# Attention: row-maximum products of 64 rows in two row groups, with the key bias added by VectorE while it takes the maximum over two PSUM banks

## The reference: what is computed

```python
def fox_block(q, k, v, fq, fk, q_pos, k_pos):
    s = jnp.einsum('bqhd,bkhd->bhqk', q, k, preferred_element_type=jnp.float32) * ATTN_SCALE
    s = s + (jnp.transpose(fq, (0, 2, 1))[..., :, None] - jnp.transpose(fk, (0, 2, 1))[..., None, :])
    mask = k_pos[None, :] <= q_pos[:, None]
    s = jnp.where(mask[None, None], s, -jnp.inf)
    p = jax.nn.softmax(s, axis=-1)
    return jnp.einsum('bhqk,bkhd->bqhd', p.astype(v.dtype), v)
```

## Time and profile before

| | |
|---|---|
| median of 3 runs | 3664.59 us (3661.96 to 3668.26) |
| the profiled execution | 3662.56 us, its span 3660.9 us |
| attention phase, first to last product | 1128.9 to 2576.0 us of the span |
| TensorE busy, share of the span | 92% |
| VectorE, ScalarE, GpSimd | 45%, 29%, 36% |

### The profile page before, as it was taken

One profiled execution on the slowest core, in us unless ns is written; L12 is line 12 of the kernel. 1 busy time (PEld: TensorE's weight loads), 2 busy tenths in 40 slices (PEclk: granted clock), 3 DMA queues, 4 the chain that ended last, 5 costly groups with the idle time before them and its releaser, 6 DMA issues. The chain is left out here.

```text
span 3660.9 us, 49247 instructions
## 1 busy us (share of the span) xinstructions
PE 3355.1 (92%) x17784; PEld 2379.2 (65%) x17784; DVE 1656.8 (45%) x2644; ACT 1073.9 (29%) x1451; POOL 1334.9 (36%) x1273
## 2 busy tenths in 40 slices
PE   7999999796965999999999999999699999959998
PEld 5777777572823666666666666665377777748877
DVE  3223332262615655555555555553334443345554
ACT  4222222131311544545444445454200000001111
POOL 0000000033331888787878787878100000000000
PEclk9999999898985999999999999999799999979999
DMA  5333334399987113132232323110311111055664
GB/s 171 122 127 115 127 119 152 120 361 373 379 321 146 41 36 82 46 72 59 58 65 59 73 47 82 35 27 10 130 46 46 57 57 69 23 157 183 206 200 158
DMA packets 238130, 435.33 MB, mean 119 GB/s; under 512 B 63543, under 2 KB 105528, under 8 KB 235871
## 3 DMA queue, kind: packets, MB, share of 16 engines
q1 hardware_dynamic: 217191, 364.96, 32.8%
q0 software_dynamic: 20768, 68.17, 4.9%
HBM read 314.19 MB, written 119.03 MB: 118 GB/s over the span
## 5 line engine op out<-in xcount | busy, mean ns | idle before, releaser
L931 DVE TENSOR_REDUCE at_max_parts<-at_mx 128x1 f32<-128x512 f32 (+3 forms) x1152 | 736.6, 646 | 411.0 <-PE at_mx L991 284.7
L874 ACT ACTIVATE at_probs<-at_st,at_gap 128x1024 f32<-128x1024 f32 x448 | 498.2, 1114 | 511.5 <-PE at_st L1021 511.2
L840 POOL TENSOR_TENSOR at_pair_sum<-at_probs 128x1024 f32<-128x1024 f32 x224 | 531.2, 2372 | 196.7 <-ACT at_probs L874 180.2
L1041 PE MATMUL at_o_ps<-at_probs,at_v 128*64 128x512 f32 (+3 forms) x2304 | 499.8, 566 | 0.0
L991 PE MATMUL at_mx<-at_k_one,at_q_top 71*128 71x512 f32 (+3 forms) x1152 | 461.8, 402 | 14.4 <-DMA at_k_all<-scratch_k_parts 8.2
L1020 PE MATMUL at_st<-at_q_all,at_k_all 128*128 128x512 f32 (+3 forms) x1152 | 459.4, 399 | 6.9 <-ACT at_probs L878 5.6
L1021 PE MATMUL at_st<-at_q_one,at_k_one 67*128 67x512 f32 (+3 forms) x1152 | 440.4, 382 | 0.0
L93 PE MATMUL ga_acc<-ga_h_high,ga_w_high 128*128 128x512 f32 x768 | 311.7, 406 | 23.3 <-DVE ga_h_low L1285 21.0
L1041 PEld LDWEIGHTS at_o_ps<-at_probs,at_v 128*64 128x64 f32 x2304 | 171.8, 137 | 246.1 <-issue 185.3
L94 PE MATMUL ga_acc<-ga_h_low,ga_w_high 128*128 128x512 f32 x768 | 307.2, 400 | 0.0
L95 PE MATMUL ga_acc<-ga_h_high,ga_w_low 128*128 128x512 f32 x768 | 307.2, 400 | 0.0
(11 more groups left out here) (305 smaller groups left out, 4992.8 us busy)
## 6 DMA issues: line engine op xcount, KB each, us to landing
dc_pages<-in_cache_k_dram SPq DMA_DIRECT2D x128, 256.0 KB, 5.5
dc_pages<-in_cache_k_dram POOLq DMA_DIRECT2D x128, 256.0 KB, 5.3
dc_pages<-in_cache_v_dram SPq DMA_DIRECT2D x128, 256.0 KB, 7.6
dc_pages<-in_cache_v_dram POOLq DMA_DIRECT2D x128, 256.0 KB, 5.3
pj_x<-in_x_prompt_dram SPq DMA_DIRECT2D x32, 512.0 KB, 4.2
scratch_h_t<-pj_h_t SPq DMA_DIRECT2D x8, 2048.0 KB, 9.7
scratch_q_parts<-pj_stage SPq DMA_DIRECT2D x32, 512.0 KB, 3.3
scratch_k_parts<-pj_stage SPq DMA_DIRECT2D x32, 512.0 KB, 2.7
```

The costliest lines, as they stand in the source:

```text
L840: chain.link(nc.gpsimd.tensor_tensor(pair, first, second, ALU.add))
L874: nc.scalar.activation(probs[:, s % RING], st[:, s % 2], ACT.Exp, bias=bias).then_inc(exp_done, 1)
L931: nc.vector.tensor_reduce(max_parts[:, b % AHEAD, t, c:c + 1], mx[:, n % 2, 0:width], AX_X, ALU.max).then_inc(bank_done, 1)
L1041: last = nc.tensor.matmul(o_ps[half * HD:(half + 1) * HD, b % 2, at:TILE], v[:, h % 2, 4 * c + own], probs[:, s % RING, half, at:TILE], st ...
```

## The change

The key bias leaves the products. A unit is now up to two key tiles wide: two products of 64 rows, one with q's high part at partitions 0 to 63 (`q_all[0:64]`, keys from `k_one`), the other with the copy at partitions 64 to 127 (`q_all[64:128]`, keys from `k_all`, whose two halves change places), into the two banks of `mx`. VectorE reads both banks in one `tensor_tensor_reduce`, which adds `k_bias` (the key bias of the head, the same row in all 128 partitions, loaded by a DMA that repeats it), writes the sum back and gives the maximum. `q_top` and its loads go. A unit that takes both banks waits for the end of the use before it. The lists of units per group are remade (at most 5, or 4 on the diagonal). `combine` becomes two operations, the second of which also applies the tile's forget sum. The memsets of `k_one[HD:P]` and `q_top` go. `f_rows` has three rows in place of four, the third the full running sum. The ring of sums has six kept slots and one passing one.

```diff
-            PER = 4 + TT
+            PER = 3 + TT
...
-                chain.link(nc.vector.tensor_scalar(f_parts[:, 2], f_ones, f_past[:], None, ALU.mult))
+                chain.link(nc.vector.tensor_scalar(f_parts[:, 2].bitcast(F32), f_sum[:], -1.0, f_past[:], ALU.mult, ALU.add))
...
-                chain.link(nc.vector.scalar_tensor_tensor(out=f_parts[:, 3], in0=f_ones, scalar=f_past[:], in1=f_parts[:, 2].bitcast(F32),
-                                                          op0=ALU.mult, op1=ALU.subtract))
...
-    SUMS = 12
+    SUMS = 6
...
+    units = [(b, t, c, min(2, row(b) + 1 - c)) for b in range(NB) for t in range(TT) for c in range(0, row(b) + 1, 2)]
+    unit_base = [sum(1 for u in units if u[0] < b) for b in range(NB + 1)]
...
-        return 7 if g >= quad_base[NT] // 2 and (on_diagonal(2 * g) or on_diagonal(2 * g + 1)) else 9
+        return 4 if g >= quad_base[NT] // 2 and (on_diagonal(2 * g) or on_diagonal(2 * g + 1)) else 5
...
+        places = {1: (4,), 2: (0, 4), 3: (0, 3, 6), 4: (0, 3, 5, 8), 5: (0, 2, 4, 6, 8)}[len(here)] if here else ()
...
+    def width_of(b, t, c, n):
+
+        return n * TILE if c + n <= row(b) else (n - 1) * TILE + (t + 1) * P
...
+    kept = [n for n in range(NQUAD) if not summed_with_next(n)]
+
+    def sum_slot(n):
+
+        return SUMS if summed_with_next(n) else kept.index(n) % SUMS
...
                 sp.dma_start(k_one[h % 2][0:HD, cols].bitcast(F32), high).then_inc(k_loaded[h % 2][c], 16)
-                sp.dma_start(k_all[h % 2][0:HD, cols].bitcast(F32), high).then_inc(k_loaded[h % 2][c], 16)
-                sp.dma_start(k_all[h % 2][HD:P, cols].bitcast(F32), low).then_inc(k_loaded[h % 2][c], 16)
+                sp.dma_start(k_all[h % 2][HD:P, cols].bitcast(F32), high).then_inc(k_loaded[h % 2][c], 16)
+                sp.dma_start(k_all[h % 2][0:HD, cols].bitcast(F32), low).then_inc(k_loaded[h % 2][c], 16)
+                if h >= 2 and c == 0:
+                    sp.wait_ge(bank_done, bank_of["unit", unit_base[(h - 1) * NT] - 1] + 1)
+                sp.dma_start(k_bias[h % 2][:, cols], io["f_rows"][h, 2:3, cols].to_broadcast([P, KCHUNK])).then_inc(k_bias_loaded[h % 2][c], 16)
...
-                sp.dma_start(q_top[0:HD, n].bitcast(F32), high).then_inc(q_loaded[n], 16)
-                sp.dma_start(q_top[MINUS:KM, n].bitcast(F32), io["f_rows"][h, 2:4, cols]).then_inc(q_loaded[n], 16)
...
-                link(nc.vector.memset(t[HD:P].bitcast(F32), -1.0))
                 link(nc.vector.memset(t[HD:HD + 1].bitcast(F32), 1.0))
-            link(nc.vector.memset(q_top[HD:P].bitcast(F32), 1.0))
-            link(nc.vector.memset(q_top[HD:HD + 1].bitcast(F32), 0.0))
...
+                if k == unit_base[b] and j % 2 == 0:
+                    dve.wait_ge(k_bias_loaded[h % 2][j // 2], (h // 2 + 1) * 16)
+                dve.wait_ge(bank_ready, bank_of["unit", k] + 1)
+                both = mx[:].rearrange("p n t -> p (n t)")[:, 0:width]
+                nc.vector.tensor_tensor_reduce(out=both, in0=both, in1=k_bias[h % 2][:, c * TILE:c * TILE + width], scale=1.0, scalar=NO_MAX,
+                                               op0=ALU.add, op1=ALU.max, accum_out=max_parts[:, b % AHEAD, t, c // 2:c // 2 + 1]).then_inc(bank_done, 1)
...
-                nc.vector.tensor_reduce(shift_w[:, b % 2, :, HD], max_parts[:, b % AHEAD, :, 0:j + 1], AX_X, ALU.max, negate=True).then_inc(shift_ready, 1)
+                nc.vector.tensor_reduce(top[:], max_parts[:, b % AHEAD, :, 0:j // 2 + 1], AX_X, ALU.max).then_inc(top_ready, 1)
+                dve.wait_ge(top_ready, b + 1)
+                nc.vector.tensor_scalar(shift_w[:, b % 2, :, HD], top[:], -1.0, base[:, h, j:j + 1], ALU.mult, ALU.subtract).then_inc(shift_ready, 1)
...
-                nc.vector.tensor_copy(den_out[:, b % 2], mx[:, bank_of["den", b] % 2, 0:P]).then_inc(bank_done, 1)
+                nc.vector.tensor_copy(den_out[:, b % 2], mx[:, 0, 0:P]).then_inc(bank_done, 1)
...
-                if n >= 2:
-                    pe.wait_ge(bank_done, n - 1)
+                if n >= 1:
+                    pe.wait_ge(bank_done, n)
...
-                last = nc.tensor.matmul(mx[:, n % 2, 0:width], q_top[0:KM, b % AHEAD, t * P:(t + 1) * P],
-                                        k_one[h % 2][0:KM, c * TILE:c * TILE + width], start=True, stop=(c < j))
-                if c == j:
-                    last = nc.tensor.matmul(mx[:, n % 2, t * P:width], ident_r[:], tri[:], start=False, stop=True)
+                bank_free(bank_of["unit", k])
+                keys = k_one[h % 2][0:HD], k_all[h % 2][HD:P]
+                for i in range(n):
+                    width = TILE if c + i < j else (t + 1) * P
+                    last = nc.tensor.matmul(mx[:, i, 0:width], q_all[i * HD:(i + 1) * HD, b % AHEAD, t * P:(t + 1) * P],
+                                            keys[i][:, (c + i) * TILE:(c + i) * TILE + width], start=True, stop=(c + i < j))
+                if c + n > j:
+                    last = nc.tensor.matmul(mx[:, n - 1, t * P:width], ident_r[:], tri[:], start=False, stop=True)
```

More of the change, by code:

```diff
@@ L585, in phase_attend @@
     RING = 8
-    SUMS = 12
+    SUMS = 6
     BIAS0 = HD + 1
     KR = HD + 3
-    MINUS = HD + 5
-    KM = HD + 7
-    ROWS_READY = 7
-    SPREAD_READY = 12
-    MASKS_READY = 17
+    ROWS_READY = 3
+    SPREAD_READY = 8
+    MASKS_READY = 13
+    NO_MAX = -3.0e38
     def head(b):
@@ L606, in phase_attend @@
     last_step = [2 * quad_base[b + 1] - 1 for b in range(NB)]
-    unit_base = [TT * quad_base[b] for b in range(NB + 1)]
+    units = [(b, t, c, min(2, row(b) + 1 - c)) for b in range(NB) for t in range(TT) for c in range(0, row(b) + 1, 2)]
+    unit_base = [sum(1 for u in units if u[0] < b) for b in range(NB + 1)]
     NGROUP = NQUAD // 2
@@ L677, in phase_attend @@
         q_all = m.sb("q_all", [P, AHEAD, TILE], F32R)
-        q_top = m.sb("q_top", [P, AHEAD, TILE], F32R)
+        k_bias = [m.sb(f"k_bias{i}", [P, SEQ]) for i in range(2)]
         q_one = m.sb("q_one", [P, AHEAD, TILE], F32R)
@@ L706, in phase_attend @@
         bias_loaded = [m.sem(f"bias_loaded{i}") for i in range(2)]
+        k_bias_loaded = [[m.sem(f"k_bias_loaded{i}_{c}") for c in range(NKC)] for i in range(2)]
         v_loaded = [m.sem(f"v_loaded{i}") for i in range(2)]
@@ L824, in end @@
                     chain.link(last)
-                    last = nc.gpsimd.tensor_tensor(quad_sum[:, n % SUMS], quad_sum[:, n % SUMS], quad_sum[:, (n - 1) % SUMS], ALU.add)
+                    last = nc.gpsimd.tensor_tensor(quad_sum[:, sum_slot(n)], quad_sum[:, sum_slot(n)], quad_sum[:, SUMS], ALU.add)
                 last.then_inc(summed, 1)
@@ L830, in add_quad @@
                 b = block_of[n]
-                out = quad_sum[:, n % SUMS]
+                out = quad_sum[:, sum_slot(n)]
                 first, second = probs[:, 2 * n % RING], probs[:, (2 * n + 1) % RING]
                 pool.wait_ge(exp_done, 2 * n + 2)
-                if n >= SUMS:
-                    pool.wait_ge(bank_ready, bank_of["den", block_of[n - SUMS]] + 1)
+                if not summed_with_next(n) and kept.index(n) >= SUMS:
+                    pool.wait_ge(bank_ready, bank_of["den", block_of[kept[kept.index(n) - SUMS]]] + 1)
                 if n + 1 < quad_base[b + 1]:
@@ L926, in unit @@
             def unit(k):
-                b, t, c = unit_at(k)
-                n = bank_of["unit", k]
-                width = TILE if c < row(b) else (t + 1) * P
-                dve.wait_ge(bank_ready, n + 1)
-                nc.vector.tensor_reduce(max_parts[:, b % AHEAD, t, c:c + 1], mx[:, n % 2, 0:width], AX_X, ALU.max).then_inc(bank_done, 1)
+                b, t, c, n = units[k]
+                h, j = head(b), row(b)
+                width = width_of(b, t, c, n)
+                if k == unit_base[b] and j % 2 == 0:
[4 more added lines that the diff above has]
+                                               op0=ALU.add, op1=ALU.max, accum_out=max_parts[:, b % AHEAD, t, c // 2:c // 2 + 1]).then_inc(bank_done, 1)
             def combine(b):
@@ L952, in _ @@
             for g in range(NGROUP):
-                units = units_in(g)
+                here = units_in(g)
                 needed = unit_base[starting(g + 1)[-1] + 1] if starting(g + 1) else 0
-                for k in units:
+                for k in here:
                     if k < needed:
@@ L1052, in total @@
                     for t in range(TT):
-                        last = nc.tensor.matmul(mx[t * 32:(t + 1) * 32, n % 2, 0:P], keep["ones"][:, 0:32], quad_sum[:, q % SUMS, t * P:(t + 1) * P],
+                        last = nc.tensor.matmul(mx[t * 32:(t + 1) * 32, 0, 0:P], keep["ones"][:, 0:32], quad_sum[:, sum_slot(q), t * P:(t + 1) * P],
                                                 start=(q == quads[0]), stop=(q == quads[-1]))
```

36 lines of the change are left out of this document (14 added, 22 removed).

## The result

The changed kernel takes **3904.8 us** (median of 4 runs, 3891.5 to 3915.1) against 3663.3 for the kernel before in the same series: ratio 1.066, 95% interval 1.062 to 1.069. The forecast was 3875 with a range of 3770 to 4020. The profiled execution of the changed kernel took 3891.5 us, its span 3889.9.

What follows compares the result with a forecast made beforehand. TensorE was taken to set the pace in the attention stage (busy 1342 of 1350 us), with the new TensorE-VectorE-TensorE loop lengthening passes. 3662.6 + 226 (stage) - 14 (setup) = 3875 us, range 3770 to 4020.

Steps and rivals of the forecast that it cites:

- The full pass: Attention stage: the closed loop TensorE, VectorE, TensorE for a pair of 512 + 512 columns takes 1.92 us.
- Side by side: Maximum products: the two 64-row products of a pair overlap, so the second adds 0 us to the loop.
- serial rival: Maximum products: the 64-row products don't run side by side, adding 109 us, for 3984 us; chance 0.18.
- Five units: Attention groups holding five units: each takes 7.67 us instead of 5.83, +1.84 over 83 groups, +153 us.
- Four units: Attention groups holding four units: each takes 6.08 us instead of 5.03, +1.05 over 49 groups, +51 us.
- Denominators: After `total` writes bank 0: the next unit waits for `copy_den`, 0.48 us later, about 57 times, +27 us.
- TensorE's own work: One pass with two score blocks: pair 0.23, blocks 0.93, two layout changes 0.30, together 1.46 us, below the loop.
- `combine` hidden: VectorE's `combine` as two operations: 0.3 us more, hidden before the next pair lands; uncovered it would cost 19 us.
- Setup: Start of the attention phase: four memsets go, 16.5 us; `k_bias` loads may give some back; taken as -14 us.
- VectorE far slower: Rival on the add with maximum: 2.44 us each, from writing back or GpSimd's SBUF use, about 4300 us; chance 0.12.
- faster: Rival: the loop never closes last, needing the add with maximum in at most 0.68 us; 3562 us, chance 0.06.
- no change: Rival: the time stays the same, with the add with maximum near 0.9 us; chance 0.02.

Runs made afterwards that it cites:

- e2: The changed kernel with both products of a unit using all 128 rows, one after the other, so the array's layout never changes for them: 3916.8 us, ratio 1.069.
- e3: The changed kernel with VectorE reading only the last 256 columns of each unit, the other maxima left out: 3776.0 us, ratio 1.030.
- e4: e3 with the two 128-row products of e2, one after the other: 3687.6 us, ratio 1.0055.
- e5: The changed kernel with one-bank units, two banks in turn, one 128-row product, the earlier unit lists, bias still on VectorE, `combine` as in e1: 3652.7 us, ratio 0.996.
- e1: The changed kernel with `combine` as one reduction again and ScalarE adding the forget sum in a copy it makes anyway: 3893.6 us, ratio 1.0615.
- e7: The changed kernel with GpSimd's additions cut to two columns, leaving out the softmax's denominators; `combine` unchanged: 3891.0 us, ratio 1.061.

## Why the prediction was right, point by point

- **The full pass**: predicted 1.92 us, measured 1.88. The terms, with the predicted ones in parentheses: products 0.50 (0.51), start of VectorE 0.04 (0.04), read 1.23 (1.22), fetch of the maximum 0.06 (0.10), start of TensorE 0.05 (0.05).
- **Side by side**: right, both start together. That refutes the serial rival. Its price for a second product in the loop, 0.23 us, is what e2 shows. e2 isn't that rival itself, since its layout changes go as well, and so it is 12 us slower than the changed kernel and not 109.
- **Five units**: predicted +1.84 a group, measured +1.79 where nothing else stands in the group. The difference is right, its two sides aren't: up to the weighted sums such a group takes 7.94 us where 7.67 were predicted, and took 6.15 before where 5.83 were reckoned. **One or two**: -5, measured -5.5.
- **Four units**: predicted +1.05, measured +0.64, so 49 x 0.41 = 20 us too much. What is off is mainly the reckoning of the kernel before: up to the weighted sums these groups took 5.83 us, not 5.03 (23 x 0.233, less 0.3), and the changed ones take 6.47, not 6.08. Which products make up the 0.80 wasn't taken apart.
- **Denominators**: predicted 0.48 each and 27 us, measured 2.28 - 1.79 = 0.49 in groups of five units, and 25.7 us of idle time ended by the copy.
- **TensorE's own work**: the term that I sized worst. Changes of layout were put at 0.15 each. Measured are 0.39 for both and not 0.30, so TensorE's work in a pass with two blocks is 1.56 and not 1.46. It hardly shows in the total, because in full pairs the loop hides it. But it turns what I called a saving inside the sum into the loss of 88 us that e3 and e4 show. The share was wrong and the sum nearly right.
- **`combine` hidden**: wrong. It isn't two short operations but one that waits for GpSimd, 0.87 us on average; about 10 us.
- **The units ahead of the first group**: the prediction counted 16 of them and gave them no price. They cost 10.5 us. Neither clock nor loads explain it, for both kernels have a granted clock of 0.50 there and keep the DMA engines equally busy; the loop does, since nothing covers it. With the short read of e3 the stretch takes 27.9 us instead of 33.1, with the two banks in turn (e5) 26.3. The first maximum also waits for `k_bias`, 1.1 us after its products have ended.
- **The first six groups**: counted as any others, 11 us; they cost 14.0. The second of them has a granted clock of 0.77 where it was 1.00.
- **Setup**: predicted -14, measured -17.4, since `k_bias` gave nearly nothing back in front of the first product.
- **What else I had not foreseen**: five groups partly at half clock (below), about 12 us, and 3 us from the phases before.
- **The signs**: the idle time ended by VectorE was to be 130 to 200 us and is 98.6, since part of each wait counts as busy. A granted clock below 1.00 in the stage was named as a sign of being wrong; it came, 0.99 on average, and the prediction had no term for it.

These make up the 22 us by which the stage missed: -20 (four units), -3 to -4 (five units), -3 (denominators), +10.5 (units ahead of the first group), +3 (first six groups), and in the groups with `spread_shift` +36 over their neighbours without it, of which `combine` is 10, the clock about 12, and some 10, in groups of four units, is there in e1 too and stays unexplained. With the setup (-3), the phases before (+3) and those behind (-5) this is the step from 3875 to the 3891.5 us of the profiled execution; the median lies another 13 us above it. The loop was forecast rightly. That the sum came so near is in part luck: some 27 us too much stand against some 50 too little.

Of the rivals, "VectorE far slower" fell (1.23 us, and no effect of GpSimd), "faster" and "no change" needed an operation of 0.68 or 0.9 us. e3 gave it 0.43 us and the kernel was still 3% slower than before: the "faster" rival, which would have come to 3562, had left the layout changes out and so had the wrong condition.

The Trainium skill, "TensorEngine Tiling (Array Packing)", section PSUM Bottleneck, says that tiling speeds up TensorE and not the evacuation of PSUM. The runs agree: the read of two banks is the largest part, 129 us.

## What to carry to other kernels

Two buffers that take turns and are then filled and read together are one buffer: put producer, reader and producer into one sum (here 1.88 us) and compare it with the work that lies between. Count the changes of layout against side-by-side products; here an isolated pair saves 0.23 us and its changes of layout cost 0.39. Price also the units that have nothing around them, at the start of a phase. A sum that comes out right doesn't prove its terms: look at both sides of each difference. When a change bundles several steps, run each alone: the part that seemed the costliest, the bias on VectorE, is free, and with a shorter setup, which gives the gain, the kernel is 0.8% faster than before.

## What the runs showed of the hardware

- **A four-element operation that waits for GpSimd.** 0.23 us without GpSimd's additions, 0.87 on average and up to 2.15 beside them; whenever it is longer than 0.23 it ends with an operation of GpSimd. The reduction before it (0.17 us) and the large operation that reads PSUM and SBUF are not touched. The Trainium skill, "SBUF — State Buffer", section SBUF: two separate sides, describes a port pair that either VectorE or GpSimd holds, taken by VectorE operations in a two-port mode or with two SBUF inputs. The rows agree for the small operation, if it runs in such a mode, and for the large one, which has one SBUF input.
- **The granted clock falls inside the stage.** Before, it read 1.00 from 1200 to 2530 us. In the changed kernel it falls to 0.50, the 1.2 GHz level, in a few groups. One fall follows the 1.30 us of idle time above; the stretches from 2304:
```profile
2304.00:2306.00 2.00, 1.31 (x6) 0.77 (x6) 1.14 (x3) 0.54 (x1) 1.92 (x2) 0.69 0.00 0
2306.00:2308.00 2.00, 2.00 (x7) 0.76 (x8) 0.78 (x2) 0.59 (x1) 1.86 (x2) 0.50 0.00 0
2308.00:2310.00 2.00, 2.00 (x10) 0.58 (x10) 0.00 (x0) 0.00 (x0) 1.86 (x2) 0.96 0.00 0
```
  The weighted sums of this group then take 4.70 us instead of 3.65. But falls also come where TensorE had only paused for 0.41, 0.49 and 0.36 us in front of three successive pairs, and a group that lies at 0.50 from its second pair to the end of its weighted sums becomes about 5.4 us longer (e1). Behind the first six, five groups of the changed kernel exceed the kernel before by more than 3.2 us (12 us over others of their kind), in e1 seven (about 27 us). That explains why e1's profiled execution was no shorter. e2, with more idle time than either (148.4 us ended by VectorE), has a mean granted clock of 1.00 from 1200 to 2760, with falls in two groups. One group, the 140th, is among those with a fall in the changed kernel, e1, e2, e3 and e7; the others differ from run to run. What makes a fall come in one group and not in the next stays open.
